# Loads moved ahead in a two-layer decoder step: the merge's tokens and left weights, and the value weights of the compression

## The chip, the cores and the metric

The kernel runs on one core of one Trainium2 chip. The metric is the device time of one execution in microseconds (us); the time of the kernel is the median of its runs, and each comparison runs the two kernels on the same chip.

## The reference

One decoder step over two layers, for a prompt of 512 tokens and a group of 8 samples with 8 new tokens each: 576 tokens of width 1024. Cut to what matters here:

```python
z = x @ w_in                                   # layer 0: 1024 -> 6960 columns
o_a = combine_dilations([...])                 # head group A: 16 heads x 64, dilated windows
kcf = concatenate([gather_pages(cc_k, page_table), kc])     # samples: cached pages, then the new rows
o_cmp, p_cmp = cmp_attend(qb, compress(kcf, pe_k, w1_k, w2_k), compress(vcf, pe_v, w1_v, w2_v), qpos)
o_slc, o_win = ...                             # head group B: selected blocks, sliding window

def compress(k, pe, w1, w2):                   # 32 rows of 64 -> 128 hidden -> 64
    kb = k.reshape(..., 32 * 64)               # + pe
    return silu(kb @ w1) @ w2

def ab_merge(o_a, o_cmp, o_slc, o_win, ga, gb, gl, w_out):
    g = sigmoid(gl)
    o_b = g[0] * o_cmp + g[1] * o_slc + g[2] * o_win
    h = concatenate([o_a * silu(ga), o_b * silu(gb)])       # tokens x 2048
    return h @ w_out                                        # 2048 x 1024

x = layer_norm(ALPHA * x + ab_merge(...))
# layer 1: gated linear recurrence, 16 heads with a 128 x 128 state, chunkwise; then its own projection and layer_norm
```

All inputs are float32. The caches and the states, moved on by the new rows, are outputs too.

## The kernel before, in words

The program runs through stages, each a block in which every engine has its own list of instructions; semaphores alone order them. A stage's loads are issued by SyncE (SP) on one hardware queue, or by GpSimd (POOL) on its own queue; each engine issues in the order of its list, and an instruction that waits holds up what stands behind it on that engine. The stages, by the trace of before: the tokens are turned (0 to 17 us), projected (to 250), the prompt attends (to 598), the samples attend in head group A while the pages are compressed (to 930), the samples attend in head group B (to 1116), the merge (to 1264), the recurrence (to 1870), the last projection.

**Turning the tokens** (`turn_tokens`, L106). SP loads the identity, five blocks of tokens, then the projection's first weights into `late` in one transfer (1.6 MB, L122), then the page table's three small loads. TensorE (PE) transposes, VectorE (DVE) copies each of ten half blocks into `xT`, and at the end waits for the page loads and computes the row numbers `page_idx` (L153), which POOL's gathers use later. The next block begins when all of this is done.

**The projection** (`project_ab`, L175). The 6960 columns come in units. A unit's prompt part is a product of 2 x 2 blocks done as seven products instead of eight; POOL forms four sums of the unit's weights for it (L598), PE uses the weights themselves for the sample rows (L380) and for the first products, and the sums from the third product on (L389, L395). All wait for the whole of a unit's weights.

**Sample attention and compression** (`attend_and_compress`, L1325). Cached keys and values of head group A stream through a ring of six slots of 1 MiB in `arena` (SP, L1434). Beside that POOL gathers the cached pages (2 MiB each, eight pairs of keys and values) and PE multiplies them with the compression weights: `hidden`, L1588, with `late` holding the key weights and `sa_w1v` the value weights. The value weights are stored twice, once in each half of the 128 partitions; SP loads both copies, one after the other, at the stage's start (L1456), ahead of its first ring loads.

**Samples of head group B** (`attend_sample_b`, L1812). Eight samples, each with its outputs copied into `sb_ob` and stored by SP (L1899, three stores a sample) to `scratch_owin` and two like it. Near the end `ahead(sp)` loads what the merge begins with: four of the sixteen 128-row tiles of the left weights and of the prompt's tokens. While the last samples run, PE has done six of the first product's 16 calls with them.

**The merge** (`merge`, L988). `h` (tokens x 2048 turned, 16 tiles of 128 x 512) times `w_out_ab` (2048 x 1024), as 2 x 2 blocks with seven products in place of eight (L1233): each is 16 calls of 128 x 512, which the trace counts as 32 instructions. With A11, A12, A21, A22 the token blocks (A11: tiles 0 to 7, first 256 tokens; A12: tiles 8 to 15, the same tokens; A21 and A22 for the other 256) and B11 (upper left), B12 (upper right), B21 (lower left), B22 (lower right) the weight blocks, PE's order is:

- first product A11·B11 onto the banks `begun`, which ACT then copies to `first` (L1091);
- second product A12·B21 onto the same banks, after that copy;
- the turns of the gated sample rows (L1274) and the sample product against all four weight blocks;
- fifth product S1·T1, T1 = B12 − B11 formed by DVE (L1133), S1 = A21 + A22 and three other token sums by DVE (L1128);
- A12·B22, then three products with T2, T3 and T4.

On SP stand in order: the rest of B11, tiles 4 to 7 of the tokens, a wait for the last sample's store (`rows_stored`), seven loads of the sample rows (L1057, L1058), tiles 8 to 15 of the tokens, B21 in two transfers of 64 partitions each, B12, B22 (two transfers of 64 partitions), the old `x`, constants and 16 MB of cache rows that are moved to outputs. ACT runs two sigmoids of the sample rows (L1087), then the copies to `first`, then copies of turned rows, in that order. DVE runs the gate work of the sample rows, then the token sums, then T1, which it writes over B11; so T1 waits for the sample product (`ys_done`). `mab_left` and `mab_hT` are the tiles for the rest of B11 and of the tokens, allocated in this stage.

Of the kernel before, what the change touches and what calls it, by code (L numbers as in the profile page):

```python
# [17 lines left out]
P = 128  # L18
# [87 lines left out]
def turn_tokens(nc, rows, xT, ident, ident_in, page_loads, page_rows, ahead):  # L106
# [3 lines left out]
    with Space(nc, "t0") as s:  # L110
# [3 lines left out]
        turn_done, copied, ident_ready, pages_ready = (s.sem(n) for n in ("turn_done", "copied", "ident_ready", "pages_ready"))  # L114
        with nc.Block() as block:
            @block.sync
            def _(sp):
                sp.dma_start(ident[:, :], ident_in).then_inc(ident_ready, 16)
                for m, r in enumerate(rows):
                    sp.dma_start(x[0:r.shape[0], m, :], r).then_inc(x_ready[m], 16)  # L120
                for to, what, sem in ahead:
                    sp.dma_start(to, what).then_inc(sem, 16)  # L122
                for to, what in page_loads:
                    sp.dma_start(to, what, allow_slow_non_contiguous=True).then_inc(pages_ready, 16)

            @block.tensor
            def _(pe):
                pe.wait_ge(ident_ready, 16)
                for m, r in enumerate(rows):
                    n = r.shape[0]  # L130
                    pe.wait_ge(x_ready[m], 16)
                    for half in range(2):
                        t = 2 * m + half
                        if t >= 4:
                            pe.wait_ge(copied, t - 3)
# [6 lines left out]
            @block.vector  # L142
            def _(dve):
                for m, r in enumerate(rows):
                    n = r.shape[0]
                    for half in range(2):
                        t = 2 * m + half
                        dve.wait_ge(turn_done, t + 1)
                        nc.vector.tensor_copy(xT[:, 4 * half:4 * half + 4, m * P:m * P + n],
                                              turned[t % 4][:, :, 0:n]).then_inc(copied, 1)  # L150
                idx, pages, per, rest = page_rows
                dve.wait_ge(pages_ready, 16 * len(page_loads))
                nc.vector.tensor_scalar(idx[:, :], pages[:, :], float(per), rest[:, 0:1], ALU.mult, ALU.add).then_inc(copied, 1)  # L153
                dve.wait_ge(copied, 2 * len(rows) + 1)


AB_UNITS = ([("b", KC, 408, 0, 0), ("b", KC + 408, 360, 0, 1)] + [("k", KA + 512 * i, 512, 0, i) for i in range(2)]
# [17 lines left out]
def project_ab(nc, xT, main, main_in, w_in, z, qT, gT, kv, kv_b, sgl, cmp_weights, pe_bias, pTc, vd, zs, ident, d, moved):  # L175
# [54 lines left out]
    with Space(nc, "pab") as s:  # L230
# [21 lines left out]
            s.sem(n) for n in ("s_done", "v_done", "exp_in", "exp_out", "gate_ready", "p_ready", "t_done", "line"))  # L252
        other_in, slot_in = s.sem("other_in"), [s.sem(f"slot_in{u}") for u in range(2)]
# [5 lines left out]
        def weights_in(engine, u):  # L259
# [3 lines left out]
            engine.wait_ge(sem, 16 * sum(len(ab_loads(w_in, AB_UNITS[x], buffer(x)[0])) for x in group))  # L263

        with nc.Block() as block:
            @block.sync
            def _(sp):
# [5 lines left out]
                load(1)  # L273
                s.clear_last(sp)
# [10 lines left out]
            def _(pe):  # L285
# [86 lines left out]
                def rows(u):  # L372

                    w, n = buffer(u)[0], width(u)
                    weights_in(pe, u)
                    if u >= 1:
                        pe.wait_ge(act_read, ACT_READS * (u - 1) + 1)
                    for k in range(KD):
                        for half in range(2):
# [111 lines left out]
            def _(dve):  # L491
# [474 lines left out]

def merge_begin(nc, ahead, ahead_in, begun):
# [11 lines left out]
def merge(nc, h, z, o_a, o_cmp, o_slc, o_win, x_prompt, x_sample, w_out, ln_g, ln_b, x1, x1T, ident, arena, ahead_in, rows_stored, loads, next_weights, kept_rows, kept_in, begun, room):  # L979
# [7 lines left out]
    with Space(nc, "mab") as s:  # L987
        HALF_K, AHEAD = MERGE_HALF, MERGE_AHEAD  # L988
        left_first, tokens_first = merge_places(arena[0])
        left_rest, right_upper = s.sb("left", [P, HALF_K - AHEAD, 512]), s.sb("right", [P, HALF_K, 512])  # L990
        left_lower, right_lower = (a[:, :].rearrange("p (k c) -> p k c", k=HALF_K) for a in arena[1:3])
        tokens_rest = s.sb("hT", [P, 16 - AHEAD, SEQ])
# [12 lines left out]
        tokens_in, left_in, right_in = ([s.sem(f"{x}_in{late}") for late in range(2)] for x in ("tokens", "left", "right"))  # L1005
# [12 lines left out]

        def lower_rows(g, c):
            return w_rows[1024 + 512 * g:1536 + 512 * g, c].rearrange("(k p) c -> p k c", p=HD)  # L1020
# [17 lines left out]
        T1, T2, T3, T4 = B11, B11, B12, B21  # L1038
# [10 lines left out]
        with nc.Block() as block:  # L1049
            @block.sync  # L1050
            def _(sp):
                sp.dma_start(left_rest[:, :, :], w_rows[AHEAD * P:HALF_K * P, LEFT].rearrange("(k p) c -> p k c", p=P)).then_inc(left_in[0], 16)
                sp.dma_start(tokens_rest[:, 0:4, :], h[4:8].rearrange("k p t -> p k t")).then_inc(tokens_in[0], 16)
# [8 lines left out]
                sp.dma_start(right_upper[:, :, :], w_rows[0:HALF_K * P, RIGHT].rearrange("(k p) c -> p k c", p=P)).then_inc(right_in[0], 16)  # L1062
                for g in range(KVB):
                    sp.dma_start(right_lower[HD * g:HD * g + HD, :, :], lower_rows(g, RIGHT)).then_inc(right_in[1], 16)
# [20 lines left out]
            def _(act):  # L1085
# [20 lines left out]
                norm.scalar(act, 0, n)  # L1106
                turn_in(0)
# [16 lines left out]
            def _(dve):  # L1124
# [20 lines left out]

                dve.wait_ge(sig_ready, 2)
# [10 lines left out]
                a11, a12, a21, a22 = fours(0, 0), fours(1, 0), fours(0, 1), fours(1, 1)  # L1157
                s1 = [S1[:, 0:4, :], S1[:, 4:8, :]]
                dve.wait_ge(ahead_in, 32)
                dve.wait_ge(tokens_in[0], 16)  # L1160
                dve.wait_ge(tokens_in[1], 16)
                token_sum(s1, a21, a22, ALU.add).then_inc(s1_ready, 1)
                dve.wait_ge(s1_ready, 1)
                token_sum(a21, a11, a21, ALU.subtract).then_inc(s3_ready, 1)
                dve.wait_ge(s3_ready, 1)
# [5 lines left out]
                dve.wait_ge(left_in[0], 16)  # L1171
                dve.wait_ge(right_in[0], 16)
                dve.wait_ge(ys_done, 1)
# [22 lines left out]
                dve.wait_ge(right_in[1], 32)  # L1196
# [5 lines left out]
                dve.wait_ge(left_in[1], 32)  # L1202
# [25 lines left out]
            def _(pe):  # L1228
# [27 lines left out]
                pe.wait_ge(left_in[0], 16)  # L1256
                pe.wait_ge(tokens_in[0], 16)
# [3 lines left out]
                pe.wait_ge(tokens_in[1], 16)  # L1261
                pe.wait_ge(left_in[1], 32)
# [13 lines left out]
                pe.wait_ge(right_in[0], 16)  # L1276
                pe.wait_ge(turn_copied, 4)
                for k in range(16):
                    if k == HALF_K:
                        pe.wait_ge(right_in[1], 32)  # L1280
# [49 lines left out]
def attend_and_compress(nc, z, cache_k, cache_v, o, on, ident, consts, arena, late, ring_in, new_in_ring,  # L1330
# [52 lines left out]
    with Space(nc, "sa") as s_:  # L1383
# [24 lines left out]
        w1_in = [w1_first_in, s_.sem("w1v_in")]  # L1408
# [9 lines left out]
        with nc.Block() as block:  # L1418
            @block.sync
            def _(sp):  # L1420
# [34 lines left out]
                for half in range(2):  # L1455
                    sp.dma_start(w1[1][HD * half:HD * half + HD, :, :], weights[1][1].rearrange("e (c d) n -> d (e c) n", d=HD)).then_inc(w1_in[1], 16)  # L1456
# [20 lines left out]
            def _(pool):  # L1477
# [4 lines left out]
                gather(x[1][:, :, :], pool_rows[1], 0, x_in[1])  # L1482
                for i in range(2, NU):
# [9 lines left out]
            def _(pe):  # L1493
# [84 lines left out]
                def hidden(n):  # L1578
                    i, f = divmod(n, QUARTERS)
                    both(pe, copied, number["C", n] + 1)  # L1580
                    if f == 0 and i < 2:
                        pe.wait_ge(w1_in[i], 32)
# [229 lines left out]
def attend_sample_b(nc, z, pools, idx, win_k, win_v, first, first_in, second, kc, vc, qd, kT_new, consts, const_ready, o_cmp, o_slc, o_win, ident, ahead, begun, begin):  # L1812
# [12 lines left out]
    with Space(nc, "sb") as s:  # L1825
# [58 lines left out]
        with nc.Block() as block:  # L1884
            @block.sync
            def _(sp):
# [22 lines left out]
                for b in (NB - 2, NB - 1):  # L1909
                    store(b)  # L1910
# [1364 lines left out]
def build(nc, d):  # L3275
    with ExitStack() as top:
# [20 lines left out]
        moved, w_first_in = sem("moved"), sem("w_first_in")  # L3297
        cmp_weights = ((d["cmp_pe_k"], d["cmp_w1_k"], d["cmp_w2_k"]), (d["cmp_pe_v"], d["cmp_w1_v"], d["cmp_w2_v"]))
        with ExitStack() as until_merge:
            late = keep(until_merge, "late", [P, 8 * D_MODEL])  # L3300
            first = [late[:, 4 * D_MODEL * u:4 * D_MODEL * (u + 1)].rearrange("p (c k) -> p c k", c=CB) for u in range(2)]
            with ExitStack() as s:
# [8 lines left out]
                with ExitStack() as s2:  # L3311
                    xT, main = keep(s2, "xT", [P, KD, TOK]), late[:, 0:7 * D_MODEL]
                    first_unit = [(to, what, w_first_in) for to, what in
                                  ab_loads(d["w_in_ab"], AB_UNITS[0], main[:, 0:4096].rearrange("p (k c) -> p k c", k=KD))]
                    turn_tokens(nc, x_rows, xT, ident, d["ident"], page_loads, (idx, pages, per, rest), first_unit)
                    n_moved, move_rows, all_moved, all_published, z_stored = project_ab(nc, xT, main, w_first_in, d["w_in_ab"], d["z"], qT, hT, kv, kv_b, sgl, cmp_weights, pe_bias, pTc, vd, zs,
                                        ident, d, moved)
# [30 lines left out]
            out_in = [sem(f"out_ahead_in{i}") for i in range(3)]  # L3348
            with ExitStack() as s:
# [18 lines left out]
                begun = [begun_banks.enter_context(nc.psum_tensor(f"begun{i}", [P, 512], F32)) for i in range(3)]  # L3368
                b_stored = attend_sample_b(nc, d["z"], slc_rows, idx, d["cache_b_win_k"], d["cache_b_win_v"], first, first_in, x_slc, kc, vc, qd, kT_new,
# [126 lines left out]
```

## Time and profile before

| | |
|---|---|
| runs | 1972.31, 1973.15, 1977.80 us; median 1973.15 |
| the profiled execution | 1970.12 us, its span 1968.3 us |
| PE (TensorE matmuls) | 1853.9 us busy, 94% of the span |
| PEld (TensorE weight loads) | 1390.3 us, 71% |
| DVE | 1148.2 us, 58% |
| ACT | 773.4 us, 39% |
| POOL | 391.0 us, 20% |
| DMA, hardware queue / software queue | 57.4% / 10.5% of 16 engines' span |

Busy time is what an engine spent in instructions; a share says how full the span was, not what bounds a stage. PE is busy almost throughout, so the time that can be saved without less work stands in PE's gaps, and in stretches in which its clock was granted below full speed (a granted clock of 1.00 is full speed). A row that names a releaser ("<-") gives what ended the wait; it is inferred.

### The profile page before, as it was taken

The numbers are of one execution on the slowest core, as the hardware profiler recorded it, in microseconds if no ns is written. First come the engines' busy times: TensorE is split into PE (matmuls) and PEld (weight loads), VectorE is DVE, ScalarE is ACT, GpSimd is POOL, SyncE is SP. The second block draws the span as 40 slices with busy tenths as digits, with TensorE's granted clock in tenths as the row PEclk, the third lists the DMA queues.
The fourth block names the chain that finished last, engine by engine and source line by source line (L and its number), as shares of the span: only waits on it lengthen the run. The fifth ranks groups of instructions, "written<-read, shape, count | busy, mean of one in ns | idle before, by whom it ended". The sixth has DMA issues, their size and how long they took to land. (4 is left out here: it accounts for less than half of the span.)

```text
span 1968.3 us, 45788 instructions
## 1 busy us (share of the span) xinstructions
PE 1853.9 (94%) x18642; PEld 1390.3 (71%) x18642; DVE 1148.2 (58%) x2781; ACT 773.4 (39%) x1641; POOL 391.0 (20%) x424
## 2 busy tenths in 40 slices
PE   7999999999997999999889869999999999999998
PEld 7988888876776777777466524577777777777533
DVE  3111131147884444442776247589889898898565
ACT  0000011148883443443376410135455555564500
POOL 5442333335770000000545010000000000000000
PEclk9999999999998999999799989999999999999999
DMA  7243322436248999996565599699999999994231
GB/s 185 82 155 90 81 79 69 79 78 175 65 172 246 411 385 370 385 376 268 202 244 199 180 273 327 186 325 307 344 341 309 349 330 306 336 326 139 73 117 43
DMA packets 223663, 443.35 MB, mean 225 GB/s; under 512 B 60352, under 2 KB 181712, under 8 KB 206816
## 3 DMA queue, kind: packets, MB, share of 16 engines
q1 hardware_dynamic: 216000, 364.57, 57.4%
q0 software_dynamic: 7456, 75.86, 10.5%
q8 instruction: 150, 2.46, 0.5%
q14 instruction: 57, 0.47, 0.1%
HBM read 413.70 MB, written 165.23 MB: 294 GB/s over the span
## 5 line engine op out<-in xcount | busy, mean ns | idle before, releaser
L2502 PE MATMUL three<-x1T,arena 128*128 128x288 f32 x768 | 202.1, 410 | 1.4 <-PEq L1049 0.9
L2502 PEld LDWEIGHTS three<-x1T,arena 128*128 128x128 f32 x768 | 145.8, 192 | 41.2 <-issue 1.1
L2825 POOL TENSOR_TENSOR rec_v_own<-rec_sV,row_own 64x512 f32<-64x512 f32 x16 | 23.5, 1469 | 679.4 <-ACT rec_sV L2757 679.4
L598 POOL TENSOR_TENSOR late<-late 128x512 f32<-128x512 f32 (+2 forms) x76 | 111.8, 1471 | 211.6 <-PE pab_bZ L380 120.8
L1653 DVE COPY sa_kT<-sa_bT 128x512 f32<-128x512 f32 x80 | 55.2, 689 | 91.8 <-PE sa_bT L1509 91.7
L879 ACT ACTIVATE ap_sc<-ap_sc,ap_nmax 128x256 f32<-128x256 f32 (+1 forms) x192 | 106.3, 556 | 4.3 <-DVE ap_nmax L903 4.2
L903 DVE CUSTOM_DVE_ANT_0 ap_sc<-ap_bS,ap_bias 128x256 f32<-128x256 f32 (+1 forms) x192 | 86.0, 485 | 15.4 <-DMA ap_bias<-in_bias_p 8.8
L1653 ACT COPY sa_kT<-sa_bT 128x512 f32<-128x512 f32 x80 | 46.9, 586 | 93.9 <-PE sa_bT L1509 93.7
L938 POOL TENSOR_SCALAR ap_sc<-ap_sc,ap_rden,sgl 128x256 f32<-128x256 f32 (+3 forms) x128 | 76.4, 606 | 29.7 <-DVE ap_rden L911 29.7
L1672 DVE COPY sa_xT<-sa_bT 128x512 f32<-128x512 f32 x64 | 43.8, 684 | 65.8 <-PE sa_bT L1574 65.5
L465 ACT COPY zs<-pab_bZ 128x128 f32<-128x128 f32 (+2 forms) x22 | 6.4, 290 | 174.5 <-PE pab_bZ L380 174.5
L2502 PE MATMUL three<-x,arena 128*128 128x288 f32 x256 | 69.5, 415 | 0.6 <-DVE rec_qq L2927 0.6
L1588 PE MATMUL sa_bH<-sa_xT,late 64*128 64x128 f32 x1024 | 66.0, 277 | 4.0 <-issue 3.6
L1588 PE MATMUL sa_bH<-sa_xT,sa_w1v 64*128 64x128 f32 x1024 | 65.3, 276 | 1.5 <-issue 0.8
L1509 PE MATMUL sa_bT<-ident,arena 64*128 64x64 f32 x1280 | 57.6, 229 | 9.6 <-ACT sa_pT_new L1664 2.5
L1588 PEld LDWEIGHTS sa_bH<-sa_xT,late 64*128 64x128 f32 x1024 | 60.5, 188 | 8.4 <-issue 7.9
L2502 PEld LDWEIGHTS three<-x,arena 128*128 128x128 f32 x256 | 47.8, 192 | 24.6 <-issue 12.4
L1509 PEld LDWEIGHTS sa_bT<-ident,arena 64*128 64x128 f32 x1280 | 51.3, 143 | 18.6 <-issue 16.7
L1588 PEld LDWEIGHTS sa_bH<-sa_xT,sa_w1v 64*128 64x128 f32 x1024 | 60.3, 188 | 5.6 <-issue 5.0
L389 PE MATMUL pab_bA<-xT,late 128*128 128x256 f32 x256 | 62.1, 386 | 0.0
L2932 DVE RECIPROCAL rec_sf<-rec_sf 128x576 f32<-128x576 f32 x16 | 60.0, 3753 | 0.6
L1672 ACT COPY sa_xT<-sa_bT 128x512 f32<-128x512 f32 x64 | 37.7, 588 | 51.6 <-PE sa_bT L1574 51.3
(593 smaller groups left out, 4503.1 us busy)
## 6 DMA issues: line engine op xcount, KB each, us to landing
out<-in_cache_a_k SPq DMA_DIRECT2D x8, 8160.0 KB, 29.0
out<-in_cache_a_v SPq DMA_DIRECT2D x8, 8160.0 KB, 29.2
arena<-in_cache_a_k SPq DMA_DIRECT2D x40, 1024.0 KB, 9.2
arena<-in_cache_a_v SPq DMA_DIRECT2D x40, 1024.0 KB, 9.5
arena<-in_w_in_c SPq DMA_DIRECT2D x64, 512.0 KB, 7.0
late<-in_w_in_ab SPq DMA_DIRECT2D x128, 64.0 KB, 2.3
late<-in_w_in_ab SPq DMA_DIRECT2D x8, 1024.0 KB, 5.2
ap_bias<-in_bias_p SPq DMA_DIRECT2D x16, 512.0 KB, 3.9
```

What stands on the lines that cost most here:

```text
L389: last = nc.tensor.matmul(bank[:, 0:HALF], left[:, k, 0:n], right[:, k, :], start=(first and k == 0), stop=(k == 3), skip_group_check=True)
L598: nc.gpsimd.tensor_tensor(to, a, b, op).then_inc(sums, 1)
L879: nc.scalar.activation(at, at, ACT.Exp, bias=nmax[:, i % RING, h:h + 1], scale=-1.0, accum_out=den[:, i % RING, h:h + 1]).then_inc(exp_don ...
L903: nc.vector.tensor_tensor_reduce(out=sc[i % RING][h][:, 0:cols], in0=bS[i % 2][h][:, 0:cols], in1=bias[grp % 2][:, h, SEQ - cols:SEQ], sca ...
L938: nc.gpsimd.tensor_scalar(at, at, rden[:, i % RING, h:h + 1], gate, ALU.mult, ALU.mult).then_inc(p_ready, 1)
L1509: last = nc.tensor.transpose(pair[half][:, n * HD:(n + 1) * HD], ring[at % RING][r, t, j * P:(j + 1) * P], ident[r, r])
L1588: last = nc.tensor.matmul(bH[g][:, 0:P], w1[i % 2][r, EACH * f + j, :], xT[r, n % QUARTERS, j, :], start=(f == 0 and j == 0), stop=(f == Q ...
L1653: copy(to, bT[n % 2][half][:, :].rearrange("p (j t k) -> p j t k", j=4, t=2)).then_inc(copied[half], 1)
L1672: copy(xT[:, n % QUARTERS, :, HD * half:HD * half + HD], bT[m % 2][half][:, :].rearrange("p (c n) -> p c n", n=HD)).then_inc(copied[half], 1)
L2502: last = nc.tensor.matmul(grouped(bank[:, 0:NT_HALF]), left[:, k, :], right[:, k, :, :], start=(first and k == 0), stop=(k == 3), skip_gro ...
L2825: nc.gpsimd.tensor_tensor(v_own[:, :, :], sV[0:TS, :].unsqueeze(1).broadcast_to([TS, HALF_NB, P]), row_own[:, :].unsqueeze(2).broadcast_to ...
L2932: line(nc.vector.reciprocal(sf[:, :], sf[:, :]))
```

## The change

Four things change.

1. *Merge.* The tile `oT`, which the last stages fill with the recurrence's outputs, is allocated from the start, and `late` becomes a part of it; so `late` outlives the stage before the merge. The rest of B11 and the rest of the tokens now have their places in `late`, B21 its old place in `arena[1]`. All three are loaded by SP in `attend_sample_b`, between the store of sample 6 and that of sample 7: `ahead_late` once sample 6 is done (`late` held key and value pages until then), `ahead_lower` once the last keys are turned. B21 and B22 come in eight pieces over all 128 partitions.
2. *Merge.* T1 goes to `x1T` (still empty then) in place of B11; it no longer waits for the sample product, which T2 now does, written over B11. ACT's first turned rows into `x1T` wait for T2. The first two token sums stand ahead of the gate work on DVE.
3. *Compression.* One copy of the value weights is loaded by SP, the other by POOL's queue, behind the first gather of value pages.
4. *Start.* DVE makes one half of the copies into `xT`, ACT the other. The first weights come in four pieces with a semaphore each, and the sample rows' product of unit 0 takes them piece by piece. The page loads are issued in the projection, and `page_idx` is computed in its unit 1.

```diff
 turn_tokens
-                for to, what in page_loads:
-                    sp.dma_start(to, what, allow_slow_non_contiguous=True).then_inc(pages_ready, 16)
...
-                dve.wait_ge(pages_ready, 16 * len(page_loads))
-                nc.vector.tensor_scalar(idx[:, :], pages[:, :], float(per), rest[:, 0:1], ALU.mult, ALU.add).then_inc(copied, 1)
...
+            @block.scalar
+            def _(act):
+                for m, r in enumerate(rows):
+                    n = r.shape[0]
+                    act.wait_ge(turn_done, 2 * m + 2)
+                    nc.scalar.copy(xT[:, 4:8, m * P:m * P + n], turned[(2 * m + 1) % 4][:, :, 0:n]).then_inc(copied[1], 1)
 project_ab
                 load(1)
+                for to, what in page_loads:
+                    sp.dma_start(to, what, allow_slow_non_contiguous=True).then_inc(pages_ready, 16)
...
                     for k in range(KD):
+                        if u == 0:
+                            pe.wait_ge((first_pieces + [main_in])[k * FIRST_PIECES // KD], 16)
...
+                    if (u, i) == (1, 2):
+                        row, pages, per, rest = page_rows
+                        dve.wait_ge(pages_ready, 16 * len(page_loads))
+                        line(nc.vector.tensor_scalar(row[:, :], pages[:, :], float(per), rest[:, 0:1], ALU.mult, ALU.add))
 new functions
+def merge_late(h, w_rows, late):
+    left, tokens = merge_late_places(late)
+    return [(left, w_rows[MERGE_AHEAD * P:MERGE_HALF * P, 0:512].rearrange("(k p) c -> p k c", p=P)),
+            (tokens[:, 0:4, :], h[4:8].rearrange("k p t -> p k t")), (tokens[:, 4:12, :], h[8:16].rearrange("k p t -> p k t"))]
+def merge_lower_rows(w_rows, k, c):
+    return w_rows[1024:2048, c].rearrange("(g k p) c -> k g p c", g=KVB, p=HD)[k]
+                def load_merge_late(sp):
+                    for (to, what), arrived in zip(merge_late(d["h"], w_out_ab, late), merge_late_in):
+                        sp.dma_start(to, what).then_inc(arrived, 16)
+                def load_merge_lower(sp):
+                    to = arena[1][:, :].rearrange("p (k c) -> p k c", c=512)
+                    for k in range(MERGE_HALF):
+                        sp.dma_start(to[:, k, :], merge_lower_rows(w_out_ab, k, slice(0, 512))).then_inc(merge_late_in[3], 16)
 attend_sample_b
                 ahead(sp)
-                for b in (NB - 2, NB - 1):
-                    store(b)
+                store(NB - 2)
+                sp.wait_ge(o_done, NB - 1)
+                ahead_late(sp)
+                wait_turns(sp, "K", NB - 1, QUARTERS - 1)
+                ahead_lower(sp)
+                store(NB - 1)
 merge
-        T1, T2, T3, T4 = B11, B11, B12, B21
+        T1_home = x1T[:, :, :].rearrange("p k t -> p (k t)")[:, 0:HALF_K * 512].rearrange("p (k c) -> p k c", c=512)
+        T1, T2, T3, T4 = [T1_home[:, k, :] for k in range(HALF_K)], B11, B12, B21
...
-                sp.dma_start(left_rest[:, :, :], w_rows[AHEAD * P:HALF_K * P, LEFT].rearrange("(k p) c -> p k c", p=P)).then_inc(left_in[0], 16)
-                sp.dma_start(tokens_rest[:, 0:4, :], h[4:8].rearrange("k p t -> p k t")).then_inc(tokens_in[0], 16)
                 rows_stored(sp)
...
-                sp.dma_start(tokens_rest[:, 4:12, :], h[8:16].rearrange("k p t -> p k t")).then_inc(tokens_in[1], 16)
-                for g in range(KVB):
-                    sp.dma_start(left_lower[HD * g:HD * g + HD, :, :], lower_rows(g, LEFT)).then_inc(left_in[1], 16)
...
+                act.wait_ge(t2_ready, 1)
                 turn_in(0)
...
+                token_sum(s1, a21, a22, ALU.add).then_inc(s1_ready, 1)
+                dve.wait_ge(s1_ready, 1)
+                token_sum(a21, a11, a21, ALU.subtract).then_inc(s3_ready, 1)
...
                 dve.wait_ge(sig_ready, 2)
                 line(nc.vector.tensor_tensor(sig[:, 1, :], sig[:, 1, :], ins[:, 1, :], ALU.mult))
...
-                dve.wait_ge(ys_done, 1)
                 weight_sum(T1, B12, B11).then_inc(t1_ready, 1)
...
-                dve.wait_ge(right_in[1], 32)
+                dve.wait_ge(right_lower_in, 16 * HALF_K)
+                dve.wait_ge(ys_done, 1)
                 weight_sum(T2, B22, T1).then_inc(t2_ready, 1)
 attend_and_compress
-                for half in range(2):
-                    sp.dma_start(w1[1][HD * half:HD * half + HD, :, :], weights[1][1].rearrange("e (c d) n -> d (e c) n", d=HD)).then_inc(w1_in[1], 16)
+                sp.dma_start(w1[1][0:HD, :, :], weights[1][1].rearrange("e (c d) n -> d (e c) n", d=HD)).then_inc(w1_in[1], 16)
...
                 gather(x[1][:, :, :], pool_rows[1], 0, x_in[1])
+                h_stored(pool)
+                pool.dma_start(w1[1][HD:P, :, :], weights[1][1].rearrange("e (c d) n -> d (e c) n", d=HD)).then_inc(w1_upper_in, 16)
```

## Rows read from the trace of the kernel before

**Rows 1.** Waits of PE, whole span: engine, line, releaser: us, times, longest.

```profile
PE begun L1233 <- DMA arena<-in_w_out_ab: 12.9, 1, 12.9
PE mab_acc_b L1233 <- DVE mab_left L1133: 5.2, 1, 5.2
PE sa_bH L1588 <- issue: 4.5, 4, 3.0
PE sa_bT L1509 <- DMA arena<-in_cache_a_k: 1.4, 1, 1.4
```

**Rows 2.** Timeline of the merge, PE: start us, us, engine, line, operation [idle before].

```profile
1124.59 9.75 PE L1233 MATMUL begun<-mab_left,mab_hT 128*128 128x512 f32 x16 [6.32 <-DMA mab_hT<-scratch_h]
```

**Rows 3.** Windows: us, PE, PEld, DVE, ACT, POOL, PEclk, DMA share, GB/s.

```profile
1132.20:1137.40 5.20, 2.14 (x5) 0.59 (x4) 2.99 (x2) 2.99 (x4) 2.98 (x1) 0.94 1.06 378
1147.20:1162.70 15.50, 15.44 (x32) 6.63 (x32) 6.93 (x6) 0.00 (x0) 0.00 (x0) 0.90 1.06 286
1183.70:1199.60 15.90, 15.90 (x32) 6.95 (x33) 9.85 (x16) 0.20 (x1) 0.00 (x0) 0.87 1.00 328
1199.60:1213.40 13.80, 13.80 (x33) 5.89 (x31) 10.91 (x18) 0.00 (x0) 0.00 (x0) 1.00 1.09 364
```

**Rows 4.** Timeline of SP's queue around the merge's start.

```profile
1102.01 0.60 SPq L1899 DMA_DIRECT2D scratch_owin<-sb_ob  x1
...
1114.93 0.60 SPq L1899 DMA_DIRECT2D scratch_owin<-sb_ob  x1
...
1121.23 0.60 SPq L1058 DMA_DIRECT2D mab_gl<-scratch_z  x1
```

**Rows 5.** DMA issues, 1095 to 1180 us: times, KB each, median us to landing.

```profile
mab_left<-in_w_out_ab SPq DMA_DIRECT2D x1, 1024.0 KB, 5.0
...
scratch_owin<-sb_ob SPq DMA_DIRECT2D x2, 32.0 KB, 1.9
...
mab_gl<-scratch_z SPq DMA_DIRECT2D x1, 12.0 KB, 11.0
```

**Rows 6.** Timeline of ACT and DVE in the merge.

```profile
1132.30 1.91 ACT L1087 ACTIVATE mab_sig<-mab_ins 64x2048 f32<-64x2048 f32 x1 [14.74 <-DMA mab_gl<-scratch_z]
1134.25 1.04 ACT L1091 COPY w_out_rows<-begun 128x512 f32<-128x512 f32 x2
...
1145.93 1.22 DVE L1153 TENSOR_TENSOR mab_ins<-mab_ins,mab_sig 64x1024 f32<-64x1024 f32 x1
1147.07 1.21 DVE L1128 TENSOR_TENSOR w_out_rows<-arena,mab_hT 128x1024 f32<-128x1024 f32 x1
```

**Rows 7.** Timeline of the start, all engines.

```profile
3.88 0.59 SPq L122 DMA_DIRECT2D late<-in_w_in_ab  x1
...
15.99 0.23 DVE L153 TENSOR_SCALAR page_idx<-pages,place_in_page 128x8 int32<-128x8 int32 x1 [2.89 <-DMA place_in_page<-in_block_of_page]
16.83 11.47 POOL L598 TENSOR_TENSOR late<-late 128x816 f32<-128x816 f32 x4 [16.39 <-POOLq L115]
...
28.45 3.00 PE L395 MATMUL pab_bC<-late,xT 128*128 128x204 f32 x16 [1.13 <-POOL late L598]
...
37.24 1.91 POOL L598 TENSOR_TENSOR gT<-gT,arena 128x816 f32<-128x816 f32 x1
```

**Rows 8.** DMA issues, 0 to 17 us.

```profile
late<-in_w_in_ab SPq DMA_DIRECT2D x1, 1632.0 KB, 11.1
```

**Rows 9.** Timeline of SP's queue, start of the compression.

```profile
609.81 5.99 SPq L1456 DMA_DIRECT2D sa_w1v<-in_cmp_w_v  x2
...
624.95 2.18 SPq L1434 DMA_DIRECT2D arena<-in_cache_a_k  x3
```

**Rows 10.** DMA issues, 598 to 640 us.

```profile
sa_w1v<-in_cmp_w_v SPq DMA_DIRECT2D x2, 1024.0 KB, 15.1
```

**Rows 11.** Windows, start of the compression.

```profile
617.70:620.70 3.00, 0.00 (x0) 0.00 (x0) 0.00 (x0) 0.00 (x0) 0.00 (x0) 1.00 1.17 176
620.70:625.10 4.40, 4.36 (x60) 2.97 (x60) 1.38 (x2) 1.17 (x2) 0.98 (x1) 0.61 1.23 180
```

More of the change, by code:

```diff
@@ L103, in pool_dma_sem, with turn_tokens @@
         return Space.kept.enter_context(self.nc.semaphore(f"{self.tag}_{name}"))
-def turn_tokens(nc, rows, xT, ident, ident_in, page_loads, page_rows, ahead):
+def turn_tokens(nc, rows, xT, ident, ident_in, ahead):
     with Space(nc, "t0") as s:
@@ L113, in turn_tokens @@
         x_ready = [s.sem(f"x_ready{m}") for m in range(TILES + 1)]
-        turn_done, copied, ident_ready, pages_ready = (s.sem(n) for n in ("turn_done", "copied", "ident_ready", "pages_ready"))
+        turn_done, ident_ready = s.sem("turn_done"), s.sem("ident_ready")
+        copied = [s.sem(f"copied{half}") for half in range(2)]
         with nc.Block() as block:
@@ L263, in weights_in @@
             engine.wait_ge(sem, 16 * sum(len(ab_loads(w_in, AB_UNITS[x], buffer(x)[0])) for x in group))
+            if u == 0:
+                for piece in first_pieces:
+                    engine.wait_ge(piece, 16)
         with nc.Block() as block:
@@ L1004, in merge @@
         spare_bank = s.bank("spare_bank")
-        tokens_in, left_in, right_in = ([s.sem(f"{x}_in{late}") for late in range(2)] for x in ("tokens", "left", "right"))
+        left_rest_in, tokens_first_in, tokens_last_in, left_lower_in = late_in
+        right_upper_in, right_lower_in = (s.sem(x) for x in ("right_upper_in", "right_lower_in"))
         in_ready, x_ready, sig_ready, ha_ready, hb_ready, pool_line, dve_line = (
@@ L1809, in attend_and_compress, with attend_sample_b @@
     return out_stored
-def attend_sample_b(nc, z, pools, idx, win_k, win_v, first, first_in, second, kc, vc, qd, kT_new, consts, const_ready, o_cmp, o_slc, o_win, ident, ahead, begun, begin):
+def attend_sample_b(nc, z, pools, idx, win_k, win_v, first, first_in, second, kc, vc, qd, kT_new, consts, const_ready, o_cmp, o_slc, o_win, ident, ahead, ahead_late, ahead_lower, begun, begin):
     NKT, TC, GONE = CB, 8, -2e4
@@ L3312, in build @@
                     xT, main = keep(s2, "xT", [P, KD, TOK]), late[:, 0:7 * D_MODEL]
[L3313 to L3317, printed above, removed]
+                    first_unit = [(to[:, 2 * k:2 * k + 2], what[:, 2 * k:2 * k + 2], w_first_in[k]) for to, what in
+                                  ab_loads(d["w_in_ab"], AB_UNITS[0], main[:, 0:4096].rearrange("p (k c) -> p k c", k=KD)) for k in range(FIRST_PIECES)]
+                    turn_tokens(nc, x_rows, xT, ident, d["ident"], first_unit)
+                    n_moved, move_rows, all_moved, all_published, z_stored = project_ab(nc, xT, main, w_first_in[-1], w_first_in[:-1], d["w_in_ab"], d["z"], qT, hT, kv, kv_b, sgl, cmp_weights, pe_bias, pTc, vd, zs,
+                                        ident, d, moved, page_loads, (idx, pages, per, rest))
                 ring_in, new_in_ring = [sem(f"ring_in{i}") for i in range(5)], sem("new_in_ring")
```

90 lines of the change are left out of this document (46 added, 44 removed).

## The prediction

> **What bounds the kernel now.** I read the waits of TensorE (PE) over the whole span first, because PE is nearly always busy and only its gaps are on offer. The reader is to see that two of the three largest gaps that this change can touch stand in the merge: 12.9 us for the lower left weights, and 5.2 us for VectorE's (DVE's) difference of weights; compression adds 4.5 us that no semaphore explains (3.0 in one piece) and 1.4 us for a block of cached keys [rows 1]. The timeline of the merge then shows the third: 6.32 us for the prompt's tokens, after which 16 instructions take 9.75 us [rows 2]. The windows give PE's own pace: 32 instructions of this form take 13.8 us at a granted clock of 1.00, 0.43 us each, but 15.5 and 15.9 us right after the other two gaps, at 0.90 and 0.87 [rows 3]. So a gap costs more than its idle time: the clock had fallen while PE idled, from the upper level of 2.4 GHz towards 1.2.
>
> The profiled execution took 1970.12 us, 1.8 more than its span of 1968.3; the median of the runs shown is 1973.15. I sum the gains against the execution and take them from the median.
>
> **The merge.** Three terms disappear in full if the loads come in time: first product 6.3 + (9.75 − 16 × 0.43) = 9.2 us; second product 12.9 + (15.5 − 13.8) = 14.6 us; fifth product 5.2 + (15.9 − 13.8) = 7.3 us; together 31.1 us.
>
> Do they come in time? The two ahead-steps go into SP's queue behind the store of sample 6, which is out at 1102.6 [rows 4]. By the tiles' shapes they move 1 MiB of left weights, 3 MiB of tokens, then 2 MiB of lower weights, the last over all 128 partitions. Tokens with 2 KB rows over all partitions moved at 378 GB/s [rows 3], and 1 MiB landed 5.0 us after its issue [rows 5], of which 2.2 us are not bytes (1.05 MB / 378 = 2.8). So left weights and tokens land by 1102.6 + 2.2 + 11.1 = 1115.9, and all 6 MiB (16.6 us) by 1121.4. PE reaches the first product at 1118.3 (1124.6 − 6.3) and leaves it at 1125.2. Its two waits are gone.
>
> What is late next is on the same queue. Sample 7's store is issued at about 1115 [rows 4] and landed in 1.9 us on a free queue [rows 5]; now it stands behind the 6 MiB and lands at about 1121.9. SP may load the sample rows only once it has landed. On the path before, the seven loads took 7.6 us of transfer (tokens landed 1124.6, the last one at 1121.2 + 11.0 = 1132.2) [rows 2, 4, 5]; so the last lands at 1121.9 + 2.2 + 7.6 = 1131.7, only 0.5 us earlier than now. ScalarE (ACT) runs in order: its sigmoids wait for those rows, and its copies of the first product stand behind the sigmoids, starting 1.95 us after them [rows 6]. The second product accumulates onto the same bank and waits for that copy: 1131.8 + 1.95 + 0.5 = 1134.3. That is a new wait of 9.1 us, and a slow start after it; the trace has 1.7, 2.1 and 2.9 us for gaps of 12.9, 5.2 and 6.3, I take 2.1. So the merge gives 31.1 − 9.1 − 2.1 = **19.9 us**.
>
> The rest hides. DVE's two token sums (four instructions of 1.21 us, 4.9 in all [rows 6]) move ahead of the gate work; the tokens have landed by 1115.9, so they end near 1121.5, long before the gates can start. The gate chain ends 14.9 us after the sigmoids start (1132.3 to 1147.2 [rows 6]), at 1146.7, while the second product runs to 1134.3 + 15.9 = 1150.2. The weight difference follows: two sums of 2.4 us, then the 5.2 us that PE waited, done by about 1158; the sample product ends 15.8 us after the second (1162.7 to 1178.5 before [rows 1, 3]), at 1166. Its new home, not the old weights, is why this wait goes. The second difference now waits for the sample product too, but is due only after the fifth product, 13.8 us later. ACT's added wait stands before copies that PE asks for after the next product. Early copies of cache rows and the next stage's weights shift forward with everything else.
>
> Bounds: if the store isn't held up by the bytes before it, the rows land some 4.5 us earlier and the merge gives 24.4; if the 6 MiB ran at half the pace, they land 16.6 us later and it gives 3.3. I take 19.9: the row for the same shape is the nearest.
>
> **The start.** Before, DVE idles from 13.1 to 16.0 for the page table, and the projection's block opens after that [rows 7]. The page loads go into the next block, where their user comes in unit 1, far from the path. But GpSimd (POOL) sets the pace: PE's third product waited for its four sums, which ran from 16.83 to 28.3 [rows 7]. POOL still needs the whole of the first weights, landing at 3.9 + 11.1 = 15.0 [rows 7, 8], four pieces or one. So it starts about 1.7 us earlier. The sums took 2.87 us each beside DVE and 1.91 alone; DVE starts earlier, by 13.6, and so leaves more of them alone: with some 2.6 sums beside it and 1.4 alone they end at 15.1 + 7.5 + 2.7 = 25.3. Gain **3.0 us**; bounds 1.7 (none faster) and 4.5 (28.3 less four at 1.91 from 15.1 would be 5.5, but PE's own two products before it take the rest). That ScalarE takes half of the copies matters only up to the moment the weights land.
>
> **Compression.** SP spent 6.0 us on issuing the two halves of the value weights, and its next key load went out only at 624.95 [rows 9]. With one half on POOL, whose gather stands before it, the keys go out several microseconds earlier: the 1.4 us wait goes. The 3.0 us gap, in which all five engines stood still, and the clock of 0.61 after it (4.4 us, some 1.8 lost) [rows 11] may go or come twice; nothing tells which. I take **1.4 us**; bounds −4.8 and 6.2.
> Beside this the Trainium skill speaks against the edit (SBUF — State Buffer, "Can I just issue two DMAs to hit both halves?"): two transfers on opposite halves of the partitions, issued at once, gained only 6% over one. By that rule the 2 MiB end where they did; the trace of before has the halves on one queue only (15.1 us each to land [rows 10]), so it can't say. The sum without this term would be 1.4 us smaller.
>
> **Sum.** 19.9 + 3.0 + 1.4 = 24.3 us; 1973.15 − 24.3 = **1948.9 us**.
>
> **Rivals.**
> (a) *The rows come early.* The store passes in time, or the 6 MiB flow faster, and the 3.0 us gap goes too: 24.4 + 3.0 + 6.2 = 33.6, 1939.6 us. For it: the queue is empty from 1103 to 1114. Against: everything is one queue.
> (b) *The halves still serialise*, and the keys wait as before: gain 22.9, 1950.3 us. For it: engines were full while they loaded (176 GB/s at a share of 1.17 [rows 11]). Against: SP's issue time shrinks anyway. This is what the skill's rule makes of the place.
> (c) *SP chokes.* Eleven issues fill the queue, SP comes late to sample 7's store, and the rows land 10 us later: gain 14.3, 1958.9 us. For it: an issue took 6 us when much was outstanding [rows 9].
> (d) *The change does nothing*: the queue at half pace as for 64-partition loads: 3.3 + 1.7 + 0 = 5.0, 1968.2 us.
> (e) *Slower.* POOL's half stands behind its 2 MiB gather and needs POOL for its issue; PE's first product with value weights at 636.9 now waits for it. Its price is 1 us per us from there; it decides from a landing about 23 us later, at 660. At 665 the kernel takes about 1978 us. Against: each half landed in 15.1 us [rows 10].
>
> **How the numbers follow.** Forecast 0.55, (a) 0.20, (b) 0.10, (c) 0.08, (d) 0.04, (e) 0.03. The forecast's own range is 1944 to 1954. The range 1938 to 1959 takes in (a) to (c) and leaves out (d) and (e). About 0.3% (5.9 us) is what a measurement can tell from no change: faster 0.93, same 0.04, slower 0.03.
>
> **What would show it.** In the changed trace: no wait of PE for tokens or lower left weights; a wait before the second product of about 9 us put down to ACT's copy; the sample rows landing near 1131 less the earlier gains; no wait before the fifth product, and 13.8 us for it; the third product of unit 0 at about 25.4; the keys issued well before 624 and no wait for them. The forecast is wrong if the second product starts right behind the first (then (a)), or if its wait exceeds 15 us (then (c)), or if PE waits for the value weights.

## The result: slower by 1.7%

The changed kernel takes 2009.46 us (median of 4 runs, 2007.13 to 2010.01) against 1975.47 for the kernel before in the same comparison: ratio 1.0167, 95% interval 1.0140 to 1.0194. The forecast was 1948.9 and its range ended at 1959. The profiled execution took 2010.01 us; its page begins with

```profile
span 2008.2 us, 45804 instructions
PE 1851.6 (92%) x18642; PEld 1388.4 (69%) x18642; DVE 1145.0 (57%) x2776; ACT 776.3 (39%) x1646; POOL 389.9 (19%) x425
```

No engine has more than 3 us of additional work; PE has 42 us more of gaps. Its waits over the span (engine, line, releaser: us, times, longest) name three that were not there:

```profile
PE begun L1284 <- PEq L1916: 35.1, 1, 35.1
PE begun L1311 <- DMA arena<-in_w_out_ab: 22.9, 1, 22.9
PE begun L1262 <- ACT w_out_rows L1118: 9.5, 1, 9.5
```

The 12.9 and 5.2 us of the merge [rows 1] and the 6.3 us for tokens [rows 2] are gone, as intended. In their place PE stands 35.1 us before the merge's block opens, 9.5 us before the second product, and 22.9 us in the middle of the sample product. The timeline of PE shows them in place:

```profile
1108.89 2.84 PE L1008 MATMUL begun<-arena 128*128 128x512 f32 x6
...
1146.81 3.35 PE L1284 MATMUL begun<-arena 128*128 128x512 f32 x4 [35.08 <-PEq L1916]
1149.99 7.03 PE L1262 MATMUL begun<-oT 128*128 128x512 f32 x16
1166.57 15.73 PE L1262 MATMUL begun<-arena,oT 128*128 128x512 f32 x32 [9.54 <-ACT w_out_rows L1118]
...
1214.08 8.96 PE L1311 MATMUL begun<-arena,mab_hs 128*64 128x512 f32 x32 [22.93 <-DMA arena<-in_w_out_ab]
1222.97 14.00 PE L1262 MATMUL mab_acc_b<-x1T,w_out_rows 128*128 128x512 f32 x32
```

The first product now takes 7.03 us where it took 9.75 [rows 2], and the fifth 14.00 with no wait where it took 15.9 [rows 3]. What opens a block is that every engine has left the one before; the queue of SP says which one had not:

```profile
1098.62 0.59 SPq L3410 DMA_DIRECT2D oT<-in_w_out_ab  x1
1099.25 1.06 SPq L3410 DMA_DIRECT2D oT<-scratch_h  x2
1100.42 37.25 SPq L3415 DMA_DIRECT2D arena<-in_w_out_ab  x8
1137.71 7.12 SPq L1931 DMA_DIRECT2D scratch_ocmp<-sb_ob  x1
1144.88 0.59 SPq L1931 DMA_DIRECT2D scratch_oslc<-sb_ob  x1
1145.51 0.60 SPq L1931 DMA_DIRECT2D scratch_owin<-sb_ob  x1
...
1158.86 36.66 SPq L1091 DMA_DIRECT2D arena<-in_w_out_ab  x8
```

Three transfers of 4 MiB in all are out in 1.7 us; the eight pieces of B21, 256 KB each, hold SP for 37.25 us, and the last store stands behind them until 1146.1. The block opens at 1146.8. The eight pieces of B22 do the same at 1158.86, which is the 22.9 us. A window on the first stretch (columns as in the windows above) shows what they move with:

```profile
1120.00:1128.00 8.00, 0.00 (x0) 0.00 (x0) 0.00 (x0) 0.00 (x0) 0.00 (x0) 0.50 0.13 51
```

No engine works, the clock granted to TensorE is at its lower level (0.50), and the sixteen DMA engines are busy to a mean share of 0.13, as much as two of them would be if they never paused. They move 51 GB/s, where prompt tokens had run at 378 [rows 3].

From the last product of head group B (1113.0 before, 1108.7 after) to the first of the recurrence's attention (1309.7, 1346.8) the kernel before needs 196.7 us and the changed one 238.1. I use this stretch below as "the merge's stretch": it leaves out what happens elsewhere. Each figure of it is from one execution.

### The profile page after: what moved, and what is told of

It reads as the page before. It is cut to its first block and busy times, and to the rows that moved or that the text cites. A ratio compares the mean times of both kernels' runs of the same rounds, so it can differ in the third digit from the quotient of the medians.

```text
span 2008.2 us, 45804 instructions
## 1 busy us (share of the span) xinstructions
PE 1851.6 (92%) x18642; PEld 1388.4 (69%) x18642; DVE 1145.0 (57%) x2776; ACT 776.3 (39%) x1646; POOL 389.9 (19%) x425
## 5 line engine op out<-in xcount | busy, mean ns | idle before, releaser
L613 POOL TENSOR_TENSOR oT<-oT 128x512 f32<-128x512 f32 (+2 forms) x76 | 110.2, 1451 | 209.2 <-PE pab_bZ L391 120.4
L1620 PE MATMUL sa_bH<-sa_xT,oT 64*128 64x128 f32 x1024 | 66.2, 277 | 3.5 <-issue 3.2
L1539 PEld LDWEIGHTS sa_bT<-ident,arena 64*128 64x128 f32 x1280 | 51.6, 143 | 21.5 <-issue 21.1
L1620 PEld LDWEIGHTS sa_bH<-sa_xT,oT 64*128 64x128 f32 x1024 | 60.7, 189 | 8.0 <-issue 7.5
L400 PE MATMUL pab_bA<-xT,oT 128*128 128x256 f32 x256 | 62.1, 386 | 0.0
```

Source lines behind the costliest of these rows:

```text
L400: last = nc.tensor.matmul(bank[:, 0:HALF], left[:, k, 0:n], right[:, k, :], start=(first and k == 0), stop=(k == 3), skip_group_check=True)
L613: nc.gpsimd.tensor_tensor(to, a, b, op).then_inc(sums, 1)
L1539: last = nc.tensor.transpose(pair[half][:, n * HD:(n + 1) * HD], ring[at % RING][r, t, j * P:(j + 1) * P], ident[r, r])
L1620: last = nc.tensor.matmul(bH[g][:, 0:P], w1[i % 2][r, EACH * f + j, :], xT[r, n % QUARTERS, j, :], start=(f == 0 and j == 0), stop=(f == Q ...
```

## The experiments

Theory W (width): a transfer runs on no more DMA engines than its outermost dimension has entries; the pieces are written "k g p c" with g = 2 outermost, so on two. Rivals: Q, that 6 MiB ahead of the last store hold the queue up in any form; P, that it is the number of transfers.

**Two transfers.** The changed kernel, B21 and B22 in the kernel before's form:

```diff
-                    for k in range(MERGE_HALF):
-                        sp.dma_start(to[:, k, :], merge_lower_rows(w_out_ab, k, slice(0, 512))).then_inc(merge_late_in[3], 16)
+                    for g in range(KVB):
+                        sp.dma_start(to[HD * g:HD * g + HD, :, :], merge_lower_rows(w_out_ab, g, slice(0, 512))).then_inc(merge_late_in[3], 16)
...
+def merge_lower_rows(w_rows, g, c):
+    return w_rows[1024 + 512 * g:1536 + 512 * g, c].rearrange("(k p) c -> p k c", p=HD)
```

> The changed kernel, with the two lower weight blocks loaded in two transfers of 64 partitions each (1 MiB), as the kernel before had them. Theory W (width): a transfer is spread over no more DMA engines than its outermost dimension has entries; the pieces of 256 KB had 2 there, moved at 51 GB/s and at a DMA share of 0.13, and all of the loss comes from that. Then B21 moves at some 210 GB/s, SP is free again by 1111, the next block begins at about 1114, the second product at about 1136 (now 1166.6; 1147.3 in the kernel before), the wait before the second lower block in the sample product is gone, and the kernel takes 1950 to 1958 us. Theory Q (queue): 6 MiB ahead of the last store hold up SP and the stores whatever their form; then SP is still stuck for more than 20 us and the kernel stays above 1985.

Measured: 1959.93 us, ratio 0.9916 (0.9889 to 0.9943). SP is held for 5.93 us by B21 (the second line is the last store), PE's longest wait stands before the second product, and a window in which only B21 moves shows every DMA engine busy:

```profile
1107.09 5.93 SPq L3415 DMA_DIRECT2D arena<-in_w_out_ab  x2
1116.11 0.58 SPq L1931 DMA_DIRECT2D scratch_ocmp<-sb_ob  x1
```

```profile
PE begun L1262 <- ACT w_out_rows L1118: 14.9, 1, 14.9
```

```profile
1120.00:1126.00 6.00, 6.00 (x15) 2.66 (x14) 4.29 (x4) 0.76 (x1) 0.00 (x0) 1.00 1.06 217
```

PE waits 0.30 us for the block and none in the sample product; the merge's stretch is 182.7 us, 14.0 less than before the change. Q falls. W's time was a little too good (1950 to 1958); the wait before the second product, 14.9 us, is longer here than the 9.5 above.

**Sixteen pieces.** Twice as many transfers, each 64 partitions by one row of 2 KB:

```diff
+                    for k in range(MERGE_HALF):
+                        for g in range(KVB):
+                            sp.dma_start(to[HD * g:HD * g + HD, k, :], merge_lower_rows(w_out_ab, g, k, slice(0, 512))).then_inc(merge_late_in[3], 16)
...
+def merge_lower_rows(w_rows, g, k, c):
+    return w_rows[1024 + 512 * g + HD * k:1024 + 512 * g + HD * k + HD, c]
```

> The changed kernel, with each lower weight block in 16 pieces of 128 KB, each of them 64 partitions by one row of 2 KB (64 entries outermost). Theory W: as fast as in two transfers, 200 GB/s or more, 1950 to 1958 us. Theory P (pieces): it is the number of transfers that holds SP up, 8 pieces took 37.3 us to issue, 16 take 70 or more; then the kernel is slower than the changed kernel, 2030 us or more.

Measured: 1958.65 us, just above W's range again, ratio 0.9925 (0.9898 to 0.9952); the stretch is 181.0. P had SP held for 70 us or more; it is held for 13.48, so not P. The block opens 4.2 us late here. SP's issues, and PE's waits before the block and before the second product:

```profile
1098.13 13.48 SPq L3417 DMA_DIRECT2D arena<-in_w_out_ab  x16
```

```profile
PE begun L1263 <- ACT w_out_rows L1119: 8.2, 1, 8.2
...
PE begun L1285 <- PEq L1917: 4.2, 1, 4.2
```

**Eight pieces alone.** The kernel before, with nothing but the form of B21 and B22 changed:

```diff
         def lower_rows(g, c):
-            return w_rows[1024 + 512 * g:1536 + 512 * g, c].rearrange("(k p) c -> p k c", p=HD)
+            return w_rows[1024:2048, c].rearrange("(g k p) c -> k g p c", g=KVB, p=HD)[g]
...
-                for g in range(KVB):
-                    sp.dma_start(left_lower[HD * g:HD * g + HD, :, :], lower_rows(g, LEFT)).then_inc(left_in[1], 16)
+                for k in range(HALF_K):
+                    sp.dma_start(left_lower[:, k, :], lower_rows(k, LEFT)).then_inc(left_in[1], 16)
```

> The kernel before, with only the form of the lower weight loads changed: eight pieces of 256 KB over 128 partitions in place of two transfers of 64 partitions, at their old places in the queue. Theory W: each block takes 37 us in place of about 10, the second product begins some 20 us later than 1147.3, the sample product waits for the other block, and the kernel takes 1995 to 2010 us with nothing moved ahead. Theory Q: without the loads ahead of the last store nothing is held up, 1970 to 1980 us.

Measured: 2037.90 us, ratio 1.0298 (1.0268 to 1.0327). The direction is W's, the size is not: I had 20 to 35 us, it is 61. Both lower blocks are waited for, one after the other on the same queue:

```profile
PE begun L1233 <- DMA arena<-in_w_out_ab: 46.6, 1, 46.6
PE begun L1282 <- DMA arena<-in_w_out_ab: 24.3, 1, 24.3
```

SP issues them in 41.6 and 43.0 us. So the form alone costs more than the whole change lost: the rest of the change gives some 17 us back (see two transfers), and with the loads put ahead the form costs 50 us in place of 61.

**Thirty-two transfers of four partitions.** The crossing test: four times as many transfers as in the changed kernel, with 4 outermost in place of 2:

```diff
+                    for i in range(32):
+                        sp.dma_start(to[4 * i:4 * i + 4, :, :], merge_lower_rows(w_out_ab, i, slice(0, 512))).then_inc(merge_late_in[3], 16)
...
+def merge_lower_rows(w_rows, i, c):
+    g, q = divmod(4 * i, HD)
+    return w_rows[1024 + 512 * g:1536 + 512 * g, c].rearrange("(k p) c -> p k c", p=HD)[q:q + 4]
```

> The changed kernel, with each lower weight block in 32 transfers of 4 partitions by 8 rows of 2 KB (4 entries outermost, 64 KB each). Theory W: four engines in place of two, so about 102 GB/s, a DMA share of about 0.25 and 20 us a block, and the kernel takes 1960 to 1985 us, faster than the changed kernel although it has four times as many transfers. Theory P: 32 pieces take longer than 8; slower than 2010 us.

Measured: 1982.73 us, ratio 1.0026 (1.0004 to 1.0048), some 28 us faster than the changed kernel by the two ratios. SP is held 25.94 us for 32 issues, where 8 took 37.25, PE waits 18.0 us for the block, and the window shows a share of 0.26 (as much as 4 of 16) and 100 GB/s:

```profile
1108.76 25.94 SPq L3416 DMA_DIRECT2D arena<-in_w_out_ab  x32
```

```profile
PE begun L1285 <- PEq L1917: 18.0, 1, 18.0
```

```profile
1125.00:1133.00 8.00, 0.00 (x0) 0.00 (x0) 0.00 (x0) 0.00 (x0) 0.00 (x0) 0.51 0.26 100
```

51, 100 and 217 GB/s at shares of 0.13, 0.26 and 1.06: some 25 GB/s an engine for 2 and 4 outermost. At 64 all engines are busy, but each moves only half as much. And where SP is the last engine to leave (the changed kernel, sixteen pieces and fours), the block opens 0.7 us after its last issue each time.

The other four start from the two transfers and ask what bounds the merge once the pieces are gone.

**ScalarE's copies first.**

```diff
+                for t in range(2):
+                    act.wait_ge(p1_done, t + 1)
+                    nc.scalar.copy(first[t], acc_a[t][:, :]).then_inc(first_copied, 1)
                 act.wait_ge(in_ready, 16 * 7)
...
-                for t in range(2):
-                    act.wait_ge(p1_done, t + 1)
-                    nc.scalar.copy(first[t], acc_a[t][:, :]).then_inc(first_copied, 1)
```

> As with two transfers of 64 partitions, and ScalarE copies the first product before its sigmoids. Theory R (the landing of the sample rows bounds this place): the second product begins within 1.5 us of the first one's end (it waited 14.9 and 8.2 us in the last two runs), but the gate work still ends some 15 us after the rows have landed, so about 5 us come back as a wait before the gated rows are turned; 2 to 4 us faster than without, 1949 to 1957 us. Theory C (the order of ScalarE's list bounds it): all of the wait is saved, 8 to 15 us faster.

Measured: 1952.02 us, ratio 0.9893 (0.9865 to 0.9920). The second product starts 1.3 us after the first one's end, and the wait comes back at the turns of the gated rows, larger than the 5 us expected:

```profile
PE mab_acc_d L1303 <- DVE mab_ins L1191: 6.2, 1, 6.2
...
PE mab_acc_b L1303 <- POOL mab_ins L1149: 4.6, 1, 4.6
```

Its stretch, 180.9 us, is 1.8 less than with two transfers, too little to tell from single executions. R holds by the waits: 14.9 us went before the second product and 10.8 came back, so the landing of the sample rows sets this place, not ACT's order.

**B21 by GpSimd's queue.** SP's queue then holds only 4 MiB ahead of the last store:

```diff
-                wait_turns(sp, "K", NB - 1, QUARTERS - 1)
-                ahead_lower(sp)
                 store(NB - 1)
...
+                wait_turns(pool, "K", NB - 1, QUARTERS - 1)
+                ahead_lower(pool)
```

> As with two transfers of 64 partitions, and GpSimd's queue loads the lower left weights, once the last keys are turned; the last store and the sample rows no longer stand behind them. Theory R: sample rows land 6 to 10 us sooner after the last store, the wait before the second product falls to 5 us or less, the kernel takes 1944 to 1953 us. Theory B (the same bytes share the engines, whatever the queue): the rows land as late as before, no difference, 1952 to 1960 us.

Measured: 1949.64 us, ratio 0.9889 (0.9859 to 0.9918); the loads of the sample rows go out 3.2 us after the last store's first issue (14.2 with two transfers on SP, so 11.0 sooner where 6 to 10 was expected), the wait before the second product is 4.3 us, the stretch 171.3, 11.4 less than with two transfers on SP. R again, against B.

```profile
PE begun L1262 <- ACT w_out_rows L1118: 4.3, 1, 4.3
```

**Both.** The last two edits together.

> Both: copies before sigmoids, lower left weights by GpSimd's queue. Theory R: no wait over 1 us before the second product and at most 4 us before the gated rows are turned; 1940 to 1950 us, the fastest so far. Theory B: as with the copies alone, 1949 to 1957 us.

Measured: 1944.32 us, ratio 0.9854 (0.9827 to 0.9882), faster than both kernels. PE goes from the first product (its end is at 1124.7) to the second without a wait; the gate work is waited for once:

```profile
1124.66 13.90 PE L1262 MATMUL begun<-arena,oT 128*128 128x512 f32 x32
...
1146.34 1.11 PE L1303 MATMUL mab_acc_d<-ident,mab_ins 64*128 64x64 f32 x8 [6.63 <-DVE mab_ins L1191]
```

That wait is above the 4 us expected: in this execution the last store came 9 us after the 4 MiB and still stood behind them, so the rows landed at 1131.2. The stretch is 175.6. So what the copies add to the move to GpSimd's queue is not shown: the stretch was 171.3 without them, and the intervals of the two ratios overlap.

**Both, without the split of the value weights.** SP loads both copies, as before:

```diff
-                sp.dma_start(w1[1][0:HD, :, :], weights[1][1].rearrange("e (c d) n -> d (e c) n", d=HD)).then_inc(w1_in[1], 16)
+                for half in range(2):
+                    sp.dma_start(w1[1][HD * half:HD * half + HD, :, :], weights[1][1].rearrange("e (c d) n -> d (e c) n", d=HD)).then_inc(w1_in[1], 16)
...
-                h_stored(pool)
-                pool.dma_start(w1[1][HD:P, :, :], weights[1][1].rearrange("e (c d) n -> d (e c) n", d=HD)).then_inc(w1_upper_in, 16)
```

> Both, and the value weights of the compression loaded by SyncE alone, as in the kernel before. If the two queues save the 1.4 us wait for keys and no more, this is 1 to 2 us slower, within the noise, and the trace shows a wait of PE for a cached key block after 630 us again. If the halves side by side are what the start of the compression hangs on, 5 us slower or more. If they only serialise, no difference and no wait.

Measured: 1945.56 us, ratio 0.9851 (0.9819 to 0.9883): no difference, and a stretch of 170.9. The three kernels with B21 on GpSimd's queue thus need 170.9 to 175.6 us, the three with B21 on SP's queue and all DMA engines busy 180.9 to 182.7. PE waits for a key block in both, 1.4 us with the split (first line) and 0.8 without it:

```profile
PE sa_bT L1539 <- DMA arena<-in_cache_a_k: 1.4, 1, 1.4
```

```profile
PE sa_bT L1538 <- DMA arena<-in_cache_a_k: 0.8, 1, 0.8
```

## Why the prediction was wrong

**The step that failed** is this one, in the second paragraph on the merge: "then 2 MiB of lower weights, the last over all 128 partitions", priced with the rest at 378 GB/s, "all 6 MiB (16.6 us) by 1121.4". The first 4 MiB did land near 1114 (the last of them 13.7 us after its issue). B21 took until about 1152: the sample rows, whose loads wait for the store behind it, were issued from 1153.9. I read the destination, 128 partitions, and took the row of the shape that looked nearest; in these runs the pace went with the smaller outermost dimension of the two sides, and on the source that is g = 2. The diff shows it in `"(g k p) c -> k g p c"`. The four experiments on the form settle this: the same bytes at the same place in the queue cost 50 us more at 2 outermost than at 64, whatever the number of transfers. At 51 GB/s the 2 MiB take 41 us where the sum had 5.5; with that alone put right, the forecast's gain of 24.3 us is a loss of some 11 (an estimate from these two paces).

The Trainium skill has the rule (DMA: Bandwidth & Descriptors, "Why a DMA increments its semaphore by 16 and not by 1"): a transfer on this queue uses the largest number of engines, up to 16, that divides the slowest dimension above one on both sides. The shares of 0.13 and 0.26 agree with it. By that rule the forecast would have been a slower kernel.

**B22 was not in the sum at all.** The diff changes its form too; I moved it nowhere and so gave it no price. It cost the 22.9 us in the sample product.

**Rival (c)** named the place, SP held by eleven issues, but its price of 10 us came from two issues that took 6 us together [rows 9], and it still had the merge gain 9.9 us, where the merge's stretch became 41.4 us longer. It left out that the next block opens only when SP has left its own: 35.1 us of PE, not a later store alone. The forecast's own condition against itself, a wait over 15 us before the second product, did not show it; that wait was 9.5.

**The other steps of the merge, with two transfers in place of eight pieces.** The waits for tokens and lower left weights go (right). The store's chain, rows to sigmoids to copies, is what is late next, with a wait of 9.1 us forecast: 14.9 us with two transfers, and 8.2 with sixteen pieces after 4.2 before the block. The same term was mis-sized here too, by less: at 217 GB/s B21 takes 9.7 us where 378 gave 5.5, and the rows' loads went out 25.0 and 23.7 us after the first of the 6 MiB, not 19.3. That the changed kernel shows 9.5 agrees by chance, since there everything is late by 30 us. The second product after that wait takes 16.6 and 16.4 us where 13.8 + 2.1 was forecast. The fifth product has no wait (right). The gain, 19.9 us forecast, is 14.0 and 15.7 on the merge's stretch. With the rows freed from B21's queue it is 25.4 and the wait 4.3, where the bound for a store that isn't held up had 24.4 and 9.1 − 4.5 = 4.6; with the copies first as well the gain is 21.1 and 25.8. So the chain was read rightly.

**The start**: 3.0 us forecast, 3.9 measured. The third product starts at 24.56 (forecast 25.4; 28.45 in [rows 7]), and the next unit 3.9 us earlier; after and before:

```profile
24.56 3.00 PE L406 MATMUL pab_bC<-oT,xT 128*128 128x204 f32 x16 [1.71 <-POOL oT L613]
...
38.52 2.98 PE L391 MATMUL pab_bZ<-arena,xT 128*64 128x204 f32 x32
```

```profile
42.42 2.98 PE L380 MATMUL pab_bZ<-arena,xT 128*64 128x204 f32 x32
```

Of this 1.8 were left when the samples' stage began (597.4 against 599.2): the prompt's attention gave 2.1 back between 416 and 480 us, at the same code. Windows on that stretch, before and after, show the same instructions of PE taking 2.35 us longer at a lower mean granted clock, 0.95 against 0.97; why the clock was lower was not tested.

```profile
419.90:481.30 61.40, 55.28 (x703) 39.73 (x704) 45.65 (x188) 50.25 (x157) 32.95 (x63) 0.97 0.64 177
```

```profile
416.00:479.50 63.50, 57.63 (x702) 41.19 (x704) 45.86 (x188) 50.23 (x157) 33.05 (x63) 0.95 0.62 171
```

**The compression**: 1.4 us forecast, not confirmed. SP's next three keys went out at 621.19 (624.95 in [rows 9]), 2.0 us earlier beside the start's 1.8: the issue of the value weights shrank from 5.99 to 1.25 us, but that of the next two small loads on SP grew from 6.80 to 10.14. The wait for keys was absent in this execution. But it was there in both of the last kernels, with the weights split and without, and the time did not move. The halves landed 17.2 us (GpSimd) and 18.0 us (SP) after their issues, which lie 8 us apart, so that both were under way for some 9 us, beside other loads; on one queue each took 15.1 [rows 10]. That agrees with the rule that I weighed there (the Trainium skill, SBUF — State Buffer, "Can I just issue two DMAs to hit both halves?"): rival (b) was right for this place, as far as one execution each and the equal times show.

## What to carry to other kernels

Before pricing a transfer by a row of the trace, compare the outermost dimension of both its sides, not the bytes or the partitions: the same 2 MiB moved at 51, 100 or 217 GB/s with 2, 4 or 64 outermost. When a load changes its form, price it even if it is not moved. And when loads are put ahead of the last issue of a block, ask how long the issuing engine is held, since in this kernel every engine waits for it at the block's end.

## What the runs showed of the hardware

- Issuing can hold the engine for most of a transfer's time: the 8 issues of B21 held SP for 37.25 of the some 52 us until it had landed, at 51 GB/s; 32 issues took 25.94 us at 100 GB/s, and with all DMA engines busy 16 took 13.48 and 2 took 5.93.
- While the pieces ran, seven eighths of the DMA engines' time was idle, and yet what stood behind them on SP's queue did not pass: the last store's data were ready at 1109.4 (VectorE's copy at 1109.06 takes 0.36), its first transfer was issued at 1137.7.
- The same code took 1106.5 to 1117.2 us to the last product of head group B in four kernels whose code differs only behind that point and in the loads put ahead shortly before it (two transfers, sixteen pieces, fours, copies first). The earliest, sixteen pieces, had the higher clock: 0.89 between 935 and 1000 us, against 0.78 to 0.79 in the other three, and 0.90 between 600 and 645 us, against 0.81 to 0.85. What lowered it is open. So a term of a few us is read on its own stretch, not on the span. The window from 935 us in sixteen pieces, then in copies first:

```profile
935.00:1000.00 65.00, 55.16 (x872) 35.23 (x870) 47.72 (x190) 36.75 (x99) 37.28 (x38) 0.89 0.62 235
```

```profile
935.00:1000.00 65.00, 53.49 (x753) 33.25 (x753) 45.86 (x176) 33.36 (x89) 36.29 (x37) 0.79 0.60 222
```
